# Trainium2: the last expert's output of a top-4 mixture-of-experts layer, and the handover to the gate projection that follows it

## What is computed

```python
def moe_ffn(h, router_w, router_b, w_up, b_up, w_down, b_down):
    top_vals, top_idx = lax.top_k(tok @ router_w + router_b, TOP_K)      # 4 of 32 experts
    gate_w = jax.nn.softmax(top_vals, axis=-1)
    ...
    gu = lax.ragged_dot(x_sorted, w_up, group_sizes) + b_up[e_sorted]
    act = (u + 1.0) * (g * jax.nn.sigmoid(SWIGLU_ALPHA * g))
    out = lax.ragged_dot(act, w_down, group_sizes) + b_down[e_sorted]
    out = out * gate_w.reshape(-1)[order][:, None]
    y = jax.ops.segment_sum(out, token_of, num_segments=n_tok)

x = x + moe_ffn(rms_norm(x, moe_norm_w), ...)
ple_gate = jax.nn.sigmoid(rms_norm(x, ple_norm_w) @ w_ple_gate)
x = x + ple_gate * (p @ w_ple_proj)
y = rms_norm(x, final_norm_w)
```

## Time and profile before

| | us |
|---|---|
| median of 3 runs | 2023.15 (2022.4 to 2023.21) |
| the profiled execution | 2020.2 |
| its span, first to last instruction | 2018.4 |
| experts on TensorE, first `up` to the end of `down(31)` | 860.8 to 1948.1 |
| gate projection, first matmul to last | 1960.5 to 2010.9 |
| after it, to the end | 7.5 |

### The profile page before, as it was taken

One profiled execution on the slowest core, in us unless ns is written; L12 is line 12 of the kernel. 1 busy time (PEld: TensorE's weight loads), 2 busy tenths in 40 slices (PEclk: granted clock), 3 DMA queues, 4 the chain that ended last, 5 costly groups with the idle time before them and its releaser, 6 DMA issues.

```text
span 2018.4 us, 39184 instructions
## 1 busy us (share of the span) xinstructions
PE 1958.3 (97%) x16293; PEld 1167.0 (58%) x16293; DVE 707.6 (35%) x1079; ACT 490.8 (24%) x741; POOL 100.7 (5%) x130
## 2 busy tenths in 40 slices
PE   6999999999999999899999999999999999999978
PEld 4777878888888888624343434343434343434346
DVE  5667778778764443521010101010101010101056
ACT  3444352543534432201010101010101010101035
POOL 2000000001010000000000000000000000000021
PEclk9999999999999999999999999999999999999999
DMA  4222232222222443499999999999999999999953
GB/s 128 74 68 79 55 82 73 63 62 62 73 63 84 146 136 107 165 369 384 406 392 406 391 406 391 406 391 406 391 405 391 403 395 394 394 399 396 389 204 114
DMA packets 204653, 511.86 MB, mean 254 GB/s; under 512 B 14213, under 2 KB 126198, under 8 KB 171830
## 3 DMA queue, kind: packets, MB, share of 16 engines
q1 hardware_dynamic: 189440, 474.78, 62.8%
q0 software_dynamic: 5888, 20.97, 3.5%
q10 hardware_dynamic: 9270, 15.35, 2.0%
HBM read 493.59 MB, written 17.37 MB: 253 GB/s over the span
## 4 chain that ended last, share of the span: by engine, by line
PE 90%; DVE 4%; ACT 2%; DMA 2%; SPq 1%; issue 1%; ACTq 0%; POOL 0%; DVEq 0%; POOLq 0%
PE psum L1892 85%; PE psum L2283 1%; PE psum L2291 1%; DMA pg_raw<-in_w_ple_gate 1%; DVE arena L1369 1%; DMA arena<-y_dram,rows_u 1%; PE psum L1954 0%; ACT w_pg_hi L1151 0%; PE psum L2062 0%; SPq L585 0%; ACT w_hi L786 0%; PE psum L2022 0%; PE psum L2007 0%; DVE residual L1817 0%; DVE w_lo L1253 0%
## 5 line engine op out<-in xcount | busy, mean ns | idle before, releaser
L1892 PE MATMUL psum<-arena 128*32 128x512 f32 (+4 forms) x11480 | 1126.6, 521 | 20.1 <-ACT arena L1120 6.3
L1892 PEld LDWEIGHTS psum<-arena 128*32 128x32 f32 (+2 forms) x11480 | 487.1, 115 | 616.2 <-issue 464.7
L1772 DVE TENSOR_SCALAR arena<-psum 128x768 f32<-128x768 f32 x32 | 30.6, 958 | 967.0 <-ACT arena L1103 967.0
L1892 PE MATMUL psum<-h_hi,w_hi 128*128 128x512 f32 x640 | 258.7, 404 | 1.3 <-DVE w_lo L1253 1.3
L1892 PE MATMUL psum<-h_hi,w_lo 128*128 128x512 f32 x640 | 249.9, 390 | 0.0
L1892 PE MATMUL psum<-h_lo,w_hi 128*128 128x512 f32 x640 | 249.3, 390 | 0.0
L1253 DVE TENSOR_TENSOR w_lo<-arena,w_hi 128x1024 fp32r<-128x1024 f32 x104 | 135.7, 1306 | 187.6 <-ACT w_hi L786 186.6
L1103 ACT ACTIVATE arena<-psum 128x768 f32<-128x768 f32 x32 | 26.0, 811 | 612.3 <-PE psum L1892 612.3
L1892 PEld LDWEIGHTS psum<-h_hi,w_hi 128*128 128x128 f32 x640 | 120.3, 188 | 33.8 <-issue 8.2
L1892 PEld LDWEIGHTS psum<-h_lo,w_hi 128*128 128x128 f32 x640 | 120.4, 188 | 26.4 <-issue 2.9
L1892 PEld LDWEIGHTS psum<-h_hi,w_lo 128*128 128x128 f32 x640 | 120.1, 188 | 25.9
(11 more groups left out here) (342 smaller groups left out, 1600.4 us busy)
## 6 DMA issues: line engine op xcount, KB each, us to landing
arena<-in_w_up SPq DMA_DIRECT2D x256, 1024.0 KB, 14.1
arena<-in_w_down SPq DMA_DIRECT2D x128, 1024.0 KB, 15.1
arena<-in_w_in SPq DMA_DIRECT2D x80, 512.0 KB, 3.9
y_dram<-arena ACTq DMA_DIRECT2D x31, 288.0 KB, 6.0
arena<-in_w_ssd_branch SPq DMA_DIRECT2D x16, 512.0 KB, 4.1
arena<-in_w_attn_branch SPq DMA_DIRECT2D x8, 512.0 KB, 4.1
arena<-in_w_out SPq DMA_DIRECT2D x8, 512.0 KB, 4.4
pg_raw<-in_w_ple_gate SPq DMA_DIRECT2D x8, 512.0 KB, 6.8
```

Source lines behind the costliest of these rows:

```text
L1772: dve.tensor_scalar(u_sb, up_psum[:, :, 1, :], 1.0 + LIMIT, 1.0 - LIMIT, ALU.min, ALU.max).then_inc(u_ready, 1)
L1892: return pe.matmul(o, l, r, start=start, stop=stop)
```

## The change

1. Half of `w_ple_gate` (pieces 0 to 3) is loaded by SP in the routing, right behind the first expert's last up weights. Pieces 4 to 7 stay where all were, without the wait for `slots_summed`. `last_hot` and `last_slots` move out of the space that pieces 0 to 3 now hold early. ScalarE splits pieces 0 to 3 before `swish(31)`, pieces 4 to 7 behind it.
2. Last `down` in full tiles: `down_last` writes all 96 rows by 1024 columns in banks 0 and 1, with 96 columns of the array for k = 0 to 5 and three 32-column strips for k = 6 and 7. The three transfers at L591 are gone.
3. Last `y` in two one-hot passes: `slots_last` holds ones instead of gate weights. ScalarE's `keep_last` rounds the result to fp32r in three pieces (`y_hi`), VectorE's new `split_last` writes what is left (`y_lo`), and `sum_last` multiplies both in fp32r. `add_last` multiplies by the gate weight (`gate_last`, three more small operations in `hot_last`).
4. Eight buffers `y_got`; gathers from the fifth on wait for the last `down`'s weights to be used, as four buffers lie there.
5. TensorE's `If(extra > 0)` stands ahead of the experts: its body holds a copy of the experts' code, and an `If(extra < 1)` holds the one that runs.
6. Order: VectorE does `gather(0, 3)`, `split_last`, `gather(3, 4)`, and `add_ple(0)` and `ple_split(2)` ahead of the last two gathers; ScalarE's `ple_split(2)` and `(3)` come one step earlier or later; `ple_turn(1)` goes into `gate(0, 1)`.

```diff
@@ SP
             load_up(0, 0, 0, 2)
+            for k in range(4):
+                sp.dma_start(w_pg_raw[k], w_ple_gate[0, k * P:(k + 1) * P, :]).then_inc(w_pg_landed, 16)
             sp.wait_ge(bias_stored, 16 * 15)
...
             sp.wait_ge(ple_projected, 2 * TT)
-            sp.wait_ge(slots_summed, 2)
-            for k in range(KT):
+            for k in range(4, KT):
                 sp.dma_start(w_pg_raw[k], w_ple_gate[0, k * P:(k + 1) * P, :]).then_inc(w_pg_landed, 16)
...
-            sp.wait_ge(y_ready, 2 * EXPERTS - 1)
-            for r in range(STRIPS):
-                sp.dma_start(y_quarter[STRIP * r:STRIP * (r + 1), :],
-                             y_out[CAP:P, r * QUARTER:(r + 1) * QUARTER]).then_inc(ple_in_landed, 16)
@@ GpSimd
-                    wait(pool, y_got_added, n - 3)
+                    wait(pool, y_got_added, n - 7)
+                    if n == 4:
+                        pool.wait_ge(down_used, KT * EXPERTS)
@@ ScalarE
             def keep_last(b):
                 act.wait_ge(down_done, b + 1)
...
+                for cols, part, last in zip(LAST_COLS, y_hi, (True, False, True)):
+                    ins = act.activation(part, psum[0:CAP, cols], ACT.Copy)
+                    if last:
+                        ins.then_inc(y_ready, 1)
...
-            rounds(2, EXPERTS, 0)
+            rounds(2, EXPERTS - 1, 0)
+            copy_act(EXPERTS - 2)
+            expert_out(EXPERTS - 3)
+            act.wait_ge(w_pg_landed, 16 * 4)
+            act.wait_ge(up_used, KT * (EXPERTS - 1) + 6)
+            for k in range(4):
+                split_gate(k)
+            swish(EXPERTS - 1)
             act.wait_ge(w_pg_landed, 16 * KT)
-            for k in range(KT):
...
+            for k in range(4, KT):
+                split_gate(k)
             copy_act(EXPERTS - 1)
             expert_out(EXPERTS - 2)
             keep_last(EXPERTS - 1)
@@ VectorE
+            def split_last():
+                for i, (cols, hi, lo) in enumerate(zip(LAST_COLS, y_hi, y_lo)):
+                    dve.wait_ge(y_ready, 2 * EXPERTS - (i == 0))
+                    ins = dve.tensor_tensor(lo, psum[0:CAP, cols], hi.bitcast(F32), ALU.subtract)
+                    if i != 1:
+                        ins.then_inc(ple_lo_ready, 1)
...
-                ins = dve.tensor_tensor(xs[:, t, :], xs[:, t, :], psum[:, b * 512:b * 512 + 1024], ALU.add)
+                ins = dve.scalar_tensor_tensor(out=xs[:, t, :], in0=psum[:, b * 512:b * 512 + 1024],
+                                               scalar=gate_last[:, t:t + 1], in1=xs[:, t, :], op0=ALU.mult, op1=ALU.add)
...
-            gather(0, 4)
+            gather(0, 3)
+            split_last()
+            gather(3, 4)
             add_last(0)
...
             rstd(1)
-            gather(10, 16)
+            gather(10, 14)
+            add_ple(0)
+            ple_split(2)
             rstd(2)
-            add_ple(0)
+            gather(14, 16)
             rstd(3)
-            ple_split(2)
             add_ple(1)
@@ TensorE
+            def down_last(i):
+                pe.wait_ge(act_copied, i + 1)
+                pe.wait_ge(u_ready, i + 1)
+                for k in range(KT):
+                    pe.wait_ge(rows_landed[k // 2], 16 * (i + 1) + 48)
+                    w = w_dn_pair[k // 2][:, k % 2, :]
+                    for half in range(2):
+                        cols = slice(half * 512, half * 512 + 512)
+                        if k < 2 * STRIPS:
+                            ins = mm(bank(half)[0:CAP], act_T[:, k, 0:CAP], w[:, cols], k == 0, False)
+                        else:
+                            for j in range(STRIPS):
+                                ins = mm(bank(half)[strip(j)], act_strip(k, j), w[:, cols], False, False)
+                    ins.then_inc(down_used, 1)
...
             pe.wait_ge(ple_copied, 2 * TT)
-            experts(0, EXPERTS)
             with pe.If(extra > 0):
-                pe.wait_ge(y_ready, 2 * EXPERTS)
+                experts(0, EXPERTS)
+                pe.wait_ge(ple_copied, 2 * TT + 2)
                 experts(EXPERTS, BLOCKS)
...
+            with pe.If(extra < 1):
+                experts(0, EXPERTS)
...
+            def sum_last(t):
+                tokens = slots_last[0:CAP, t * P:(t + 1) * P]
+                for i, n in ((0, 0), (0, 1), (1, 0), (1, 1), (0, 2), (1, 2)):
+                    if t == 0 and i and n < 2:
+                        pe.wait_ge(ple_lo_ready, KT + n + 1)
+                    b, cols = SUM_BANK[t] * 512, LAST_COLS[n]
+                    ins = mm(psum[:, b + cols.start:b + cols.stop], tokens, (y_hi, y_lo)[i][n], i == 0, i == 1)
+                ins.then_inc(ple_projected, 1)
...
                for k in range(KT):
+                    if turned and k == 3:
+                        ple_turn(turned)
...
+            gate(0, 0)
+            gate(0, 1, 1)
```

More of the change, by code:

```diff
@@ L1170, in _ @@
                                    ).then_inc(ple_copied, 1)
+                for half in range(2):
+                    ins = act.activation(psum[0:CAP, half * 512:half * 512 + 512], y_kept[half][0:CAP], ACT.Copy)
+                ins.then_inc(ple_copied, 1)
             def x_summed(t):
@@ L2319, in act_strip, with down @@
                 return act_T[:, k, strip(j)] if k < 2 * STRIPS else act_T[:, 2 * j + k - 2 * STRIPS, strip(STRIPS)]
-            def down(i, base=3):
+            def down(i):
                 pe.wait_ge(act_copied, i + 1)
-                if base == 3:
-                    wait(pe, y_ready, 2 * i)
-                if base == 3 and isinstance(i, int) and i == 0:
+                wait(pe, y_ready, 2 * i)
+                if isinstance(i, int) and i == 0:
                     pe.wait_ge(ple_copied, 2 * TT + 1)
-                if base == 0:
-                    pe.wait_ge(u_ready, i + 1)
-                main, side = bank(base + 1), bank(base + 2, QUARTER)
                 for k in range(KT):
-                    pe.wait_ge(w_dn_landed[k // 2], 16 * (i + 1))
+                    pe.wait_ge(rows_landed[k // 2], 16 * (i + 1) + 48)
                     if k == KT - 1:
@@ L2335, in down @@
                     for j in range(STRIPS):
-                        mm(main[strip(j)], act_strip(k, j), w[:, 0:512], k == 0, False)
+                        mm(bank(4)[strip(j)], act_strip(k, j), w[:, 0:512], k == 0, False)
                     for j in range(2):
-                        mm(bank(base + j, QUARTER)[strip(STRIPS)], act_strip(k, j), w[:, WIDE:D], k == 0, False)
+                        mm(bank(3 + j, QUARTER)[strip(STRIPS)], act_strip(k, j), w[:, WIDE:D], k == 0, False)
                     for j in range(STRIPS):
-                        mm(side[strip(j)], act_strip(k, j), w[:, 512:WIDE], k == 0, False)
@@ L2346, in down @@
+                    mm(bank(5, QUARTER)[strip(j)], ones_bf[32:64, strip(j)], bias_dn[32:64, 0:QUARTER], False, True)
                 for j in range(2):
-                    mm(bank(base + j, QUARTER)[strip(STRIPS)], ones_bf[0:32, strip(STRIPS)], bias_dn[0:32, WIDE:D], False, True)
-                ins = mm(side[strip(STRIPS)], ones_bf[32:64, strip(STRIPS)], bias_dn[32:64, QUARTER:2 * QUARTER],
+                    mm(bank(3 + j, QUARTER)[strip(STRIPS)], ones_bf[0:32, strip(STRIPS)], bias_dn[0:32, WIDE:D], False, True)
@@ L2349, in down @@
+                ins = mm(bank(5, QUARTER)[strip(STRIPS)], ones_bf[32:64, strip(STRIPS)], bias_dn[32:64, QUARTER:2 * QUARTER],
                          False, True)
+                ins.then_inc(down_done, 1)
+            def down_last(i):
+                pe.wait_ge(act_copied, i + 1)
+                pe.wait_ge(u_ready, i + 1)
+                for k in range(KT):
+                    pe.wait_ge(rows_landed[k // 2], 16 * (i + 1) + 48)
+                    w = w_dn_pair[k // 2][:, k % 2, :]
+                    for half in range(2):
+                        cols = slice(half * 512, half * 512 + 512)
[5 more added lines that the diff above has]
+                    ins.then_inc(down_used, 1)
+                pe.wait_ge(bias_dn_landed, 32 * (i + 1))
+                for half in range(2):
+                    ins = mm(bank(half)[0:CAP], ones_bf[0:32, 0:CAP], bias_dn[0:32, half * 512:half * 512 + 512], False, True)
@@ L2376, in experts @@
                 turn_act(end - 1, last=True)
-                down(end - 1, 0 if first == 0 else 3)
+                (down if first else down_last)(end - 1)
             pe.wait_ge(tables_ready, 2)
@@ L2404, in ple_turn @@
                     pe.wait_ge(y_got_added, TOPK * (t + 1))
-                wait(pe, ple_lo_ready, KT + t)
+                pe.wait_ge(ple_lo_ready, KT + 2 + t)
                 for k in range(KT):
@@ L2409, in ple_turn, with gate @@
                 ins.then_inc(xn_turned, 1)
-            def gate(t, half):
-                pe.wait_ge(ple_lo_ready, KT + t + 1)
+            def gate(t, half, turned=None):
+                pe.wait_ge(ple_lo_ready, KT + 2 + t + 1)
                 if t >= 2:
```

(17 more changed lines are left out.)

81 lines of the change are left out of this document (41 added, 40 removed).

## The result

The changed kernel takes **2010.75 us** (median of 4 runs, 2009.08 to 2011.36) against 2022.78 for the kernel before (4 runs, 2022.3 to 2023.21): 12.0 us less, a ratio of 0.9941 with a 95% interval of 0.9927 to 0.9955. The forecast was 2014.0 with a range of 2011.0 to 2018.4.

A forecast was written before the change was run, and what follows sets the result against it. TensorE bounds the experts' rounds without idle time, so gains must come at their two ends: -5.5 + 1.4 - 2.7 - 3.3 + 0.9 = -9.2 us, from median 2023.15 to 2014.0 us, range 2011.0 to 2018.4.

The forecast's parts named there:

- ScalarE's splits: Ahead of the last down: with pieces 0 to 3 split before `swish(31)`, `down_last` begins earlier, -5.5 us.
- The last down: `down_last` in full tiles takes 14.5 us in place of 13.06, +1.4 us.
- The three strips of k = 6 and 7: Rival in `down_last`: these strips run one after the other, 7.0 us later, 2021.0 us; chance 0.07.
- From the last down to the gate: Between the end of `down_last` and `gate(0, 0)`: 9.7 us in place of 12.4, VectorE being the chain, -2.7 us.
- the store of expert 30: Ahead of `split_last`: landing 0 to 3.5 us later, 1.2 taken; late-gathers rival 2016.3 us, chance 0.13.
- the upper bound of +3.5: In `sum_last`: fp32r with 256 columns at the full float32 rate would cost up to 3.5 us more; 0 taken.
- The gates: Gate stage: eight buffers and the new order remove both TensorE pauses that VectorE ends, -3.3 us.
- The start: Start of the experts: the conditional's jump, moved there, delays the first rows, +0.9 us, bounds 0 and 3.8.
- the bound of 3.8: Start of the experts: a second fetch behind `If(extra < 1)` costs 3.8 in place of 0.9, 2016.9 us; chance 0.12.
- the 1.1 us of the jump: End of the kernel before: 1.1 us of the 2.81 us jump lay behind ScalarE's copies, on the path.
- The slower loop: Rival in the expert rounds: the loop's back edge costs an exposed fetch, 2043 at 1.0 us a round; chance 0.04.
- The low end of the range: 2011.0 us: the start at 0, the gathers at their best and 1 us of small terms.

The follow-up runs named there:

- The two experiments on the load: Changed kernel with `w_ple_gate` loaded as before, 2016.85 us; and with the early load kept but all eight splits behind `swish(31)`, 2010.74 us.
- the two experiments that left a jump bare: Changed kernel with TensorE's branch ahead of the last `turn_act`, 2014.94 us; and with strips, float32 sums and the branch at the end, 2009.79 us.

## Where the prediction was right, and which steps failed

The stretches that the change touches gave -9.9 us for a forecast of -9.2. Part of that nearness is luck: the two terms that were mis-sized most, -4.3 for -2.7 and +2.0 for +0.9, err in opposite ways.

**ScalarE's splits, forecast -5.5, measured -5.4.** The pause went from 6.30 to 0.90 us. One step inside was wrong and cost nothing: pieces 4 to 7 were to land by 1912.4, and the last landed near 1920.9, 15.8 us after its issue and not the 6.7 of the earlier trace rows (the last of the eight had taken 15.4 in the kernel before); their splits still ended 4.4 us ahead of `copy_act(31)`. The two experiments on the load show the mechanism as written, and that the load was all of it.

**The last down, +1.4 against +1.6.** 14.68 us for a forecast of 14.5. The three strips of k = 6 and 7 ran side by side; that rival is out.

**From the last down to the gate, -2.7 against -4.3.** This is the larger mis-sized term, and the step of it that failed is the store of expert 30, which the sum put 1.2 us late. Issued at 1931.93, it had its third row's addition begun at 1944.26, 12.3 us later, as in the kernel before (12.1): its two halves landed in 2.6 and 3.4 us, near the 2.5 of the earlier trace rows. So `split_last` waited for ScalarE's `y_hi` alone and began 0.7 us after the last down, not 1.7. VectorE's chain from there took 7.43 us and not 8.0: 1.35, 1.22, 3.67 and 1.14 where 1.45, 1.3, 3.9 and 1.2 were taken. fp32r matmuls of 256 columns come every 0.12 us: the upper bound of +3.5 had no part in it.

**The gates, -3.3 against -3.85.** The two pauses went. Some of the other 0.6 is the end of each pause: a matmul's record is 0.39 us long, but the next begins 0.23 after it, so a pause costs 0.16 more than its idle time. I have not followed the rest.

**The start, +0.9 against +2.0.** The early 2 MB did not hold up the gather, 4.59 us to landing against 4.49. The conditionals did, and by more than forecast; this step failed too: the first rows were turned 8.3 us after S, where 5.8 stood and 6.7 were forecast. The jump was to begin behind the load of `extra`, at 856.28 or 3.8 us after S. But TensorE first waits for `ple_copied`, the last ScalarE copy of the embeddings, and that came 4.66 us after S (3.16 in the kernel before), as the last three matmuls ahead of it (six records) took 4.33 us at half clock and not the 2.82 of the kernel before. That copy, in ScalarE's timeline of the changed kernel and above it of the kernel before:

```profile
855.01 0.60 ACT L1082 ACTIVATE embedded<-psum 128x512 f32<-128x512 f32 x1 [1.12 <-PE psum L1892]
```

```profile
855.34 0.60 ACT L1089 ACTIVATE embedded<-psum 128x512 f32<-128x512 f32 x1 [1.68 <-PE psum L1927]
```

Then the pair of conditionals took 3.67 us, not 2.8. In the eight traces with the branch at the start it took 3.6 to 4.2, and S to U was 60.4 to 61.1; in the five others S to U was 56.1 to 59.2. 0.5 us came back in the two `up`s, 23.51 and 20.81 us against 22.42 and 22.37. So the start lies between the 0.9 that I took and the bound of 3.8: the rows of 2.8 and 2.9 were for one conditional each, and I gave the second nothing. What the move was to save is the 1.1 us of the jump that lay on the path at the end; the two runs with the conditional back there show that with the full tiles nothing of it lies on the path anyway.

The Trainium skill's page "Runtime: NRT & Kernel Launch", section "Instruction fetch mechanics", says that a branch taken to a target outside the pages at hand must fetch before it can go on. The 3.6 to 4.2 us here, and the 3.90 and 4.35 us in the two experiments that left a jump bare, agree with it; that it can also be hidden for the most part, behind `down_last`, only the runs show.

**The slower loop.** U to T is 1017.8 us in both traces: the loop's place within a conditional's body costs nothing. That rival is out.

**From the sum to the time, and the range.** By these terms alone the time would have been near 2013.2, inside the range. The step that took it out is the one from the profiled execution to the median: the kernel before had its median 2.95 us above the profiled execution (2.58 with its fourth run), the sum carried that over as it stood, and in the changed kernel it was 1.67. Another 1.2 us are the untouched stretch to S. Both are the width of one execution against another: S alone moves by 2.7 us between traces, the medians of the kernel before were 2020.01 to 2022.78 in four sets of runs (those of the changed kernel's two sets differ by 0.14). The low end of the range was a sum of the costs at their best and had no room for this. The measured difference of medians is 12.0 us, and its interval reaches from 9.1 to 14.8.

## What to carry to other kernels

Price a conditional on TensorE by what is queued ahead of it: behind full-tile matmuls of 0.44 us a pass it showed for 0.9 us at most and cost nothing on the path; behind short ones it left 2.8 to 4.35 us bare, and ahead of the first work of a stage it made that work 2.3 to 3.0 us late, plus what the clock took afterwards. What of a bare jump is paid depends on what TensorE would have waited for there anyway. When a stage waits for an engine that waits for a load, ask first whether loading a part of it earlier is enough; here half of it was worth 6 us, and the order of ScalarE's splits nothing. Give the range the width of the medians, and of one profiled execution against its median, on top of the bounds of the costs.

## What the runs showed that was not expected

- **The routing's last matmuls ran at half clock in every changed kernel.** The last three float32 matmuls ahead of `ple_copied` (six records) took 4.28 to 4.52 us in all thirteen traces and 2.82 in the one trace of the kernel before. The early load isn't the cause: the kernel without it has 4.39. What is, I have not found.
- **The clock fell behind `down_last` in some traces only.** Two with full tiles and the branch at the end had 0.77 and 0.50 in 1945 to 1950, after pauses of 1.2 and 2.05 us; a third, after 1.9 us, and the changed kernel, after 1.2, had 1.00. The length of the pause alone doesn't tell them apart. After pauses of 4.7 and 4.35 us `down_last` was at 0.50 in both traces. Whether the bare jump also grows with the load on the DMA (2.8 us in the kernel before, 3.90 with gathers and 4.35, for two conditionals, with loads under way) was not separated from what is queued ahead of it.
